# A hybrid encoder block on one core: two engines' instruction orders around the first up products, and a buffer of its own for one set of token sums

## What is computed

```python
def reference(x, w_in, w_out, attn_norm_w, mlp_norm_w, ...):
    u = _rmsnorm(h, attn_norm_w[layer])
    qa, ka, va, hq, hff, hfb, hi, hg = jnp.split(u @ w_in[layer], ...)
    y_na = _neighbourhood_attention(qa, ka, va, ...)
    y_hg = _hgrn2_bidirectional(hq, hff, hfb, hi, hg, ...)   # norm, then times silu(hg)
    h = h + jnp.concatenate([y_na, y_hg], axis=-1) @ w_out[layer]
    u = _rmsnorm(h, mlp_norm_w[layer])
    a = jnp.square(jax.nn.relu(u @ w_up[layer]))
    return h + a @ w_down[layer]
```

## Time and profile before

| what | us |
|---|---|
| median of 3 runs | 1368.54 |
| lowest and highest of them | 1366.41, 1369.21 |
| the profiled execution | 1367.6 |
| its span, from the first to the last instruction | 1365.8 |
| TensorE busy (matmuls) | 1302.9 |
| VectorE busy | 910.1 |
| ScalarE busy | 582.7 |
| GpSimd busy | 488.6 |

### The profile page before, as it was taken

How to read it: one execution, slowest core, us unless ns; L and a number is a source line. 1 busy time by engine, 2 the same in 40 slices (tenths; PEclk the granted TensorE clock), 3 DMA queues, 4 the chain that set the end, 5 groups by cost and what they waited for, 6 DMA issues and landing times.

```text
span 1365.8 us, 18052 instructions
## 1 busy us (share of the span) xinstructions
PE 1302.9 (95%) x6624; PEld 1094.8 (80%) x6624; DVE 910.1 (67%) x1250; ACT 582.7 (43%) x1034; POOL 488.6 (36%) x260
## 2 busy tenths in 40 slices
PE   5998999999999999989998999999999999999998
PEld 4976777898888888878786778888888788888887
DVE  5455677641597786975756655555554888888885
ACT  6235656544443443333144544554454343233341
POOL 5232211123322132211613444444443455445452
PEclk9999999999999999999999999999999999999999
DMA  8341332222110111023420264444548844353433
GB/s 240 123 115 31 72 91 78 74 68 75 45 31 16 32 32 31 16 93 139 124 87 22 91 197 162 137 147 154 162 136 305 298 154 156 104 206 122 139 94 137
DMA packets 138533, 154.93 MB, mean 113 GB/s; under 512 B 11472, under 2 KB 97744, under 8 KB 138448
## 3 DMA queue, kind: packets, MB, share of 16 engines
q1 hardware_dynamic: 132976, 147.04, 33.6%
q10 hardware_dynamic: 5472, 6.75, 1.5%
HBM read 109.72 MB, written 44.04 MB: 113 GB/s over the span
## 4 chain that ended last, share of the span: by engine, by line
PE 84%; DVE 9%; issue 3%; ACT 3%; DMA 1%; POOL 0%; ACTq 0%; DVEq 0%
PE bank L2165 8%; PE bank L2169 7%; PE bank L2168 7%; PE bank L2134 7%; PE bank L2137 7%; PE bank L2138 7%; PE bank L1882 5%; PE bank L1886 5%; PE bank L1885 5%; PE bank L1966 4%; PE bank L2093 2%; PE bank L2097 2%; PE bank L2096 2%; PE bank L1869 2%; PE bank L1873 2%
## 5 line engine op out<-in xcount | busy, mean ns | idle before, releaser
L813 POOL TENSOR_TENSOR w_hi<-stage,one_col 128x1024 fp32r<-128x1024 f32 x36 | 71.5, 1986 | 460.6 <-PE bank L1882 346.0
L868 POOL TENSOR_TENSOR a_split<-a_raw,a_split 128x1024 fp32r<-128x1024 f32 x56 | 148.1, 2661 | 166.5 <-ACT a_split L1136 166.5
L2134 PE MATMUL bank<-set,w_hi 128*128 128x512 f32 x448 | 180.1, 402 | 5.5 <-DVE s L1705 2.6
L2137 PE MATMUL bank<-set,w_hi 128*128 128x512 f32 x448 | 177.8, 397 | 0.0
L2138 PE MATMUL bank<-set,w_lo 128*128 128x512 f32 x448 | 177.6, 397 | 0.0
L2165 PE MATMUL bank<-w_hi,a_split 128*128 128x512 f32 x448 | 174.6, 390 | 0.2
L2169 PE MATMUL bank<-w_hi,a_split 128*128 128x512 f32 x448 | 174.3, 389 | 0.0
L2168 PE MATMUL bank<-w_lo,a_split 128*128 128x512 f32 x448 | 174.3, 389 | 0.0
L1882 PE MATMUL bank<-uT_hi,w_hi 128*128 128x512 f32 x384 | 160.8, 419 | 6.5 <-DVE h_gate L1370 6.4
L1886 PE MATMUL bank<-uT_hi,w_lo 128*128 128x512 f32 x384 | 151.6, 395 | 0.0
L1885 PE MATMUL bank<-uT_lo,w_hi 128*128 128x512 f32 x384 | 151.0, 393 | 0.0
(11 more groups left out here) (208 smaller groups left out, 2832.7 us busy)
## 6 DMA issues: line engine op xcount, KB each, us to landing
a_raw<-a_dram SPq DMA_DIRECT2D x56, 512.0 KB, 3.7
a_dram<-abuf SPq DMA_DIRECT2D x111, 256.0 KB, 2.1
stage<-in_w_in SPq DMA_DIRECT2D x32, 512.0 KB, 4.2
raw<-in_w_down SPq DMA_DIRECT2D x10, 1024.0 KB, 8.1
stage<-in_w_up SPq DMA_DIRECT2D x16, 512.0 KB, 5.3
raw_b<-in_w_up SPq DMA_DIRECT2D x16, 512.0 KB, 5.5
x_tok<-in_x SPq DMA_DIRECT2D x8, 512.0 KB, 5.4
v_dram<-vs ACTq DMA_DIRECT2D x32, 128.0 KB, 1.8
```

The costliest lines, as they stand in the source:

```text
L868: pool.tensor_tensor(split_of(m, 1), a_raw[:, m % 4, :, :], split_of(m, 0).bitcast(F32), ALU.subtract).then_inc(b_lo, 1)
L2134: first = pe.matmul(dst, w[0], u[0], start=k == 0 and p in (1, 5, 6, 7), stop=False, skip_group_check=True)
L2137: pe.matmul(dst, w[0], u[1], start=False, stop=False, skip_group_check=True)
```

## The change

It has five parts; none adds or removes arithmetic.

1. `chain_states` takes the directions as an argument, and the gate's `finish_gate` stands between the two directions instead of behind both.
2. The three `mixer_lo` pairs of the output projection are made one subtraction at a time, before adds 9 to 14 (n = 8 to 13).
3. `UP_SEQ` begins (0, 1), (1, 1), (0, 2), (1, 2). Tiles 8 and 9 are turned in (0, 2) in place of (1, 1), tile 27 behind the second k-step of (1, 6) in place of the third. ScalarE's `keep_p1(1)` moves ahead of `up_weights(5)`, `take_c11(0)` and `take_set(8)`; `take_set(27)` ahead of `up_weights(13)`.
4. T2 goes to `abuf`, parts 1 to 4, instead of over T1. So it no longer waits for T1's tiles, and VectorE makes it and T4 among the reads of tiles 8 to 13. `act_sums(0)`, which writes there, waits until 24 tiles are turned.
5. `up_results(0)` stands ahead of `take_set(26)`, `take_set(27)` and the weight sum of (1, 3). From block 2 on, the weight sum for (j + 1, 6) stands behind `up_results(j)` instead of ahead of it.

```diff
-UP_SEQ = [(0, 1), (0, 2), (1, 1), (1, 2), (0, 7), ...
+UP_SEQ = [(0, 1), (1, 1), (0, 2), (1, 2), (0, 7), ...
-TURNED_AT = {(1, 1, 2): 8, (1, 1, 3): 9, (1, 2, 0): 10, ...
+TURNED_AT = {(0, 2, 2): 8, (0, 2, 3): 9, (1, 2, 0): 10, ...
...
-             (1, 5, 0): 22, ..., (1, 6, 0): 26, (1, 6, 2): 27}
+             (1, 5, 0): 22, ..., (1, 6, 0): 26, (1, 6, 1): 27}
...
+        def t2_part(t):
+            return abuf[:, 1 + t, :]
...
+            keep_p1(1)
             up_weights(5)
             take_c11(0)
-            take_set(8)
-            take_set(9)
-            keep_p1(1)
-            for g in range(10, 16):
+            for g in range(8, 16):
                 take_set(g)
...
                     if i == 8:
-                        chain_states(h)
+                        chain_states(h, (0,))
                     for n in last:
                         finish_gate(n)
+                    if i == 8:
+                        chain_states(h, (1,))
...
-                if n in (8, 20, 26):
-                    mixer_lo({8: 1, 20: 2, 26: 3}[n])
+                if 8 <= n < 14:
+                    mixer_lo(1 + (n - 8) // 2, (n % 2,))
...
+            def t2_sums(t):
+                dve.wait_ge(t13_sum, 2 * t + 1)
+                dve.tensor_tensor(t2_part(t), u_tok[:, 4 + t, HALF:D], u_tok[:, t, 0:HALF], ALU.subtract).then_inc(t2_sum, 1)
+            def t4_sums(t):
+                high = u_tok[:, t, HALF:D]
+                dve.wait_ge(y_turned, 8)
+                dve.wait_ge(t2_sum, t + 1)
+                dve.tensor_tensor(high, high, t2_part(t), ALU.subtract).then_inc(t4_sum, 1)
...
             up_results(0)
+            take_set(26)
             take_set(27)
+            up_sum(13)
             up_results(1)
...
-                    for p in (7, 5, 6):
+                    for p in (7, 5):
                         up_sum(UP_AT[(j + 1, p)])
                 up_results(j)
                 if j + 1 < UPS:
-                    up_sum(UP_AT[(j + 1, 3)])
+                    for p in (6, 3):
+                        up_sum(UP_AT[(j + 1, p)])
...
+                    src = t2_part(t)[:, P * k:P * k + P] if p == 6 else u_tok[:, t0 + t, at_:at_ + P]
...
+                if (j, p) == (1, 1):
+                    pe.wait_ge(y_lo, 5)
```

More of the change, by code:

```diff
@@ L59 @@
 UP_ORDER = (1, 7, 5, 6, 2, 4, 3)
-UP_SEQ = [(0, 1), (0, 2), (1, 1), (1, 2), (0, 7), (1, 7), (0, 5), (1, 5), (0, 6), (1, 6), (0, 4), (0, 3), (1, 4), (1, 3)]
+UP_SEQ = [(0, 1), (1, 1), (0, 2), (1, 2), (0, 7), (1, 7), (0, 5), (1, 5), (0, 6), (1, 6), (0, 4), (0, 3), (1, 4), (1, 3)]
 UP_SEQ += [(j, p) for j in range(2, UPS) for p in UP_ORDER]
@@ L66 @@
 SET_BANK = (4, 5, 6, 7, 4, 5, 6, 7, 1, 5, 3, 7, 1, 5, 0, 1, 5, 0, 1, 5, 0, 1, 5, 0, 5, 0, 0, 1)
-TURNED_AT = {(1, 1, 2): 8, (1, 1, 3): 9, (1, 2, 0): 10, (1, 2, 1): 11, (1, 2, 2): 12, (1, 2, 3): 13, (0, 7, 0): 14,
+TURNED_AT = {(0, 2, 2): 8, (0, 2, 3): 9, (1, 2, 0): 10, (1, 2, 1): 11, (1, 2, 2): 12, (1, 2, 3): 13, (0, 7, 0): 14,
              (0, 7, 1): 15, (0, 7, 2): 16, (0, 7, 3): 17, (1, 7, 0): 18, (1, 7, 1): 19, (0, 5, 2): 20, (0, 5, 3): 21,
-             (1, 5, 0): 22, (1, 5, 1): 23, (0, 6, 0): 24, (0, 6, 1): 25, (1, 6, 0): 26, (1, 6, 2): 27}
+             (1, 5, 0): 22, (1, 5, 1): 23, (0, 6, 0): 24, (0, 6, 1): 25, (1, 6, 0): 26, (1, 6, 1): 27}
 UP_BANK = {1: 0, 2: 0, 6: 1, 7: 2, 4: 2, 5: 3, 3: 3}
@@ L1256, in _ @@
             up_weights(12)
+            take_set(27)
             up_weights(13)
-            take_set(27)
             up_weights(14)
@@ L1502, in take_level, with chain_states @@
                                         bank[2 + cg][:, :].rearrange("p (c i) -> p c i", c=4)).then_inc(lev_taken, 1)
-            def chain_states(h):
+            def chain_states(h, ds):
                 dve.wait_ge(decayed, NHALF * (h + 1))
@@ L1508, in chain_states @@
                     dve.wait_ge(o_done, 2 * h)
-                for d in range(2):
+                for d in ds:
                     for j in range(2):
@@ L1534, in head_result, with mixer_lo @@
                                              ALU.mult, ALU.mult).then_inc(o_norm, 1)
-            def mixer_lo(b):
-                for f in range(FBLK):
+            def mixer_lo(b, fs=range(FBLK)):
+                for f in fs:
                     k = FBLK * b + f
@@ L1674, in _ @@
             normalise_tokens(1, TT - 1)
-            for g in range(8, 16):
-                take_set(g)
-            dve.wait_ge(y_turned, 16)
+            for t in range(3):
+                t2_sums(t)
+            take_set(8)
+            t2_sums(3)
+            take_set(9)
             for t in range(4):
-                low = u_tok[:, t, 0:HALF]
-                dve.tensor_tensor(low, u_tok[:, 4 + t, HALF:D], low, ALU.subtract).then_inc(t2_sum, 1)
-            for g in range(16, 20):
+                take_set(10 + t)
+                t4_sums(t)
+            for g in range(14, 20):
                 take_set(g)
@@ L1685, in _ @@
             up_sum(9)
-            for t in range(4):
-                dve.wait_ge(t2_sum, t + 1)
-                high = u_tok[:, t, HALF:D]
-                dve.tensor_tensor(high, high, u_tok[:, t, 0:HALF], ALU.subtract).then_inc(t4_sum, 1)
             for g in range(20, 24):
@@ L1692, in _ @@
             up_sum(11)
-            for g in range(24, 27):
-                take_set(g)
-            up_sum(13)
+            take_set(24)
+            take_set(25)
             def up_results(j):
@@ L1729, in act_sums @@
                         dve.wait_ge(a_store[i], 16 * j)
+                else:
+                    dve.wait_ge(y_turned, 24)
                 dve.tensor_tensor(a[S1], a[A21], a[A22], ALU.add).then_inc(a_sum, 1)
@@ L1846, in turn_set @@
                     at_ = col + P * k
-                    ins = pe.transpose(bank[SET_BANK[g]][:, P * t:P * t + P], u_tok[:, t0 + t, at_:at_ + P], ident)
+                    src = t2_part(t)[:, P * k:P * k + P] if p == 6 else u_tok[:, t0 + t, at_:at_ + P]
+                    ins = pe.transpose(bank[SET_BANK[g]][:, P * t:P * t + P], src, ident)
                 ins.then_inc(y_turned, 1)
```

## The result

The changed kernel takes 1347.87 us (median of 4 runs, 1346.88 to 1353.49) against 1368.88 (4 runs, 1366.41 to 1371.03) for the kernel before on the same chip: a ratio of 0.9854, 95% interval 0.9832 to 0.9877. The forecast was 1347.8. In a second set, of five runs, the changed kernel's median was 1349.6. The profiled execution took 1348.62 us, with a span of 1346.8 against 1365.8. TensorE is busy for 1297.3 us, VectorE for 888.7, ScalarE for 579.3, GpSimd for 488.1.

A forecast was written before the change was run, and what follows sets the result against it. TensorE bounds the kernel, busy 1302.9 of 1365.8 us, so only its idle time and clock can give. Gains 3.9 + 3.2 + 9.5 + 4.1 = 20.7 us, off the median of 1368.54, give 1347.8 us; range 1344.8 to 1355.

The forecast's parts named there:

- Part 1: Last head, piece 8: reading the gate's bank between the chains saves 2.5 us of TensorE wait and 1.4 of low clock.
- Part 2: Output projection: single subtractions remove waits of 2.04 and 0.79 us and about 0.35 for restarts, 3.2 us in all.
- Up to (0, 3): From the end of product (0, 1) to the start of (0, 3): 39.2 instead of 48.7 us, a gain of 9.5.
- The wait at tile 8: New TensorE wait in product (0, 2) for GpSimd's last T sum, beside VectorE's T2: 1.5 us, bounds 0.9 to 2.1.
- the work of 36.2 us: Between products (0, 1) and (0, 3): ten products, 27.5 us, and 20 turned tiles, 8.7 us, the same before and after.
- exclusive lock: At tile 8: each GpSimd sum could wait for one T2, 1.2 us in all instead of 0.7; gain then 9.0.
- Block 2: Product (2, 4)'s wait of 2.59 us for u3 goes: 2.7 us with the restart plus 1.4 of clock, 4.1 in all.
- The clock: TensorE's clock falls to mostly 1.2 GHz behind each idle time over 2.3 us, costing about 1.4 us each time.
- The low clock behind a short wait: Rival: waits of 1.5 and 0.9 us within 8 us lower the clock, 1.4 us once or twice; 1350 to 1352, chance 0.15.
- The wait at (2, 4): Rival: block 2's weight load comes late, u2 is late again and the wait stays; 1352 to 1356, chance 0.12.
- The slower rival: Blocks 2 to 14: product 3's weight sum makes VectorE stand about 2.6 us each, 34 us on top; 1382, chance 0.03.
- no wait of 2 us or more: Sign: TensorE has no such wait between piece 8 of the last head and block 3 in the profile after.

The follow-up runs named there:

- 4.1 alone: The kernel before with only the gate's bank read moved between the two chains of states in the last head's piece 8: 1365.17 us against 1368.73, ratio 0.9972.
- the turns: Traces of the changed kernel where VectorE's T2 and GpSimd's T sums alternate: three T2 in 4.05 us, sums 1.68 and 1.59; tile 8 waits 1.44 us.
- the long form: Traces of the changed order where VectorE makes all three T2 in 1.89 us while GpSimd's sum stands, 2.85 us long; tile 8 waits 2.29 us.
- 4.35 alone: The kernel before with only the weight sum for (j + 1, 6) put behind the results of block j, from block 2 on: 1362.17 us, ratio 0.9959.
- the reverse: The changed kernel with the weight sum for (j + 1, 6) ahead of the results of block j again, from block 2 on: 1353.78 us, one run.
- part 2 alone: The kernel before with only the six low-part subtractions standing singly ahead of adds 9 to 14 of the output projection: 1365.67 us, ratio 0.9975.

## Why the prediction was right

The mechanism held: the waits went where they were said to go, and each of the four sums came within 0.4 us of the traces. That the median came within 0.1 us of the forecast is luck. The four runs lie 6.6 us apart, the interval of the ratio is 3 us wide to either side, and the sum counts falls of the clock that come only in some executions.

**Part 1** was forecast at 3.9 us and gave 2.48 + 1.35 in the two traces and 4.1 alone. The reading that the gate's data are ready long before they are read held to 0.1 us: the sigmoid ended at 608.39, the read began at 608.48.

**Part 2**: 3.2 forecast, 3.4 measured, twice. A single subtraction took 1.22 us (1.17 forecast), and no new wait came.

**Up to (0, 3)**: from the end of (0, 1), at 716.90 us, it takes 39.6 us; 39.2 was forecast. The terms were less exact than their sum. The wait at tile 8 was 1.44 us (1.5 forecast) and that at (0, 7) 0.64 (0.9); those at (0, 6) and (0, 4), 0.3 each, don't show above 0.2. The waits are thus some 0.8 us less than forecast, and the work of 36.2 us, in which I counted no restarts, some 1.2 more.

The Trainium skill's exclusive lock (page "SBUF — State Buffer", section "SBUF: two separate sides") was set in the prediction at 1.2 us for the two sums, against 0.7 from the rows. Measured were 0.70 in the turns and 2.29 - 0.74 = 1.55 in the long form. Whole instructions that wait for whole instructions, as the page has it, is what both forms show (in the turns the three T2 are 0.68, 1.78 and 1.75 us long, beside the sums of 1.68 and 1.59), but how often VectorE comes first in a row it doesn't tell. My upper bound for tile 8, 2.1 us with both sums fully behind VectorE's, was passed in two of five traces.

**Block 2**: 4.1 us forecast, with 4.2 as the upper bound; 3.9 in the two traces, 4.35 alone, 4.6 in the reverse. The slack of 0.4 us came out as a wait of 0.19.

**The clock** was the weak step, though its sum held. I took each wait over 2.3 us, and only those, to bring a fall, at 1.4 us each. The first is a matter of chance at three of the five places (13 falls in 23 waits in piece 7, at tile 19 and at tile 27), and the wait of 1.8 us near 250 us brought a fall in 5 of 14 traces. The second is true only where nothing behind is waiting for another engine: at tile 19 it is 0.4. The profiled execution of before happened to show a fall at all five. In the trace with part 2 alone it didn't fall at tiles 19 and 27; there the way from M1 to u2 of block 3 is 179.46 us against 184.83, which is 1.9 us less than part 2's 3.4 explain. Read from such a trace, the forecast gain would have been smaller by about that.

**The rivals.** The low clock behind a short wait came about in one of two executions of the changed kernel, in another form than I gave it: the wait was 2.29 us, not 1.5. That fall cost 1.6 us with the longer wait, where I had said 1.4 and more. The place near 250 us speaks for this rival more than I allowed, since there waits of 1.3 and 1.8 us within 5 us do bring a fall in some executions. The wait at (2, 4) did not stay in any trace with the sum behind. The slower rival's wait of VectorE was measured at 2.07 us a block (2.6 forecast) and cost nothing, for the reason given: 5.4 us of spare time in a block. Of the signs, "no wait of 2 us or more" held in the first trace of the changed kernel and failed in the second. There the clock also fell behind tile 8, which the prediction had named as a sign of being wrong. For tile 8 it was wrong in that execution, by 0.8 us of wait over its 1.5.

## What to carry to other kernels

A wait of the bounding engine that sits behind queued work of another engine can be priced from the trace to some tenths, if one follows which instruction is late next; the parts then add. Where two engines slow each other, as VectorE and GpSimd at tile 8, the price of a meeting is not one number (0.70 and 1.55 us here): look at it in more than one trace, and bound it by the whole run of back-to-back instructions of the other engine. Count a fall of the clock as a chance, and only for what isn't covered by a wait behind it, and look for falls behind shorter waits elsewhere in the trace before you take a length of wait as harmless.
